# RMS norms with sums by token: root and inverse of 128x5, and rows made from the column by the identity

## The reference

```python
def rmsnorm(x, g):
    y = x * lax.rsqrt(jnp.mean(x * x, axis=-1, keepdims=True) + EPS)
    return y * g

def trunk_layer(x, pe, ...):
    h = x + 0.5 * rmsnorm(swiglu(rmsnorm(x, f1_pre), f1_up, f1_down), f1_post)
    mix, new = token_mix(rmsnorm(h, m_pre), ...)
    h = h + rmsnorm(mix, m_post)
    h = h + 0.5 * rmsnorm(swiglu(rmsnorm(h, f2_pre), f2_up, f2_down), f2_post)
    e = pe @ ple_w
    return h + rmsnorm(e * jax.nn.sigmoid(rmsnorm(h, ple_pre) @ ple_gate_w), ple_post), new
```

## Time and profile before

| | us |
|---|---|
| median of 3 runs | 3309.02 (3308.73 to 3309.1) |
| the profiled execution's own time | 3304.53 |
| its span | 3302.8 |
| mean granted TensorE clock | 0.975 |
| TensorE busy, matmuls / weight loads | 3122.4 / 2985.0 |
| VectorE / ScalarE / GpSimd busy | 1243.8 / 1110.9 / 1215.3 |
| norm sums L610, the group with `sq` | 86.2 in 260 instructions |
| reciprocals of norms L787 | 62.9 in 32 instructions |

### The profile page before, as it was taken

How to read it: one execution, slowest core, us unless ns; L and a number is a source line. 1 busy time by engine, 2 the same in 40 slices (tenths; PEclk the granted TensorE clock), 3 DMA queues, 4 the chain that set the end, 5 groups by cost and what they waited for, 6 DMA issues and landing times.

```text
span 3302.8 us, 55137 instructions
## 1 busy us (share of the span) xinstructions
PE 3122.4 (95%) x23487; PEld 2985.0 (90%) x23487; DVE 1243.8 (38%) x1435; ACT 1110.9 (34%) x1544; POOL 1215.3 (37%) x564
## 2 busy tenths in 40 slices
PE   8999989899999899999899999898999998999988
PEld 7999989886799899998899999888867998999977
DVE  4332134744443433212443221349344424332134
ACT  3333232235433333323433322322354333333233
POOL 5433442231143433344343334423212434333433
PEclk9999999999999999999999999999999999999998
DMA  3222222221122122232112222122211221222221
GB/s 107 83 83 80 82 59 65 73 74 47 39 77 81 54 83 83 81 89 68 58 58 84 81 81 85 54 66 72 68 47 45 77 82 52 83 83 87 82 63 48
DMA packets 455954, 236.22 MB, mean 72 GB/s; under 512 B 18630, under 2 KB 454150, under 8 KB 455814
## 3 DMA queue, kind: packets, MB, share of 16 engines
q1 hardware_dynamic: 445792, 227.05, 23.5%
q10 hardware_dynamic: 10022, 7.15, 0.7%
HBM read 228.53 MB, written 5.63 MB: 71 GB/s over the span
## 4 chain that ended last, share of the span: by engine, by line
PE 85%; DVE 8%; ACT 3%; POOL 1%; issue 1%; ACTq 1%; POOLq 0%; DVEq 0%
PE ps L585 77%; PE ps L610 3%; DVE ps L787 2%; PE ps L1487 1%; DVE uf L799 1%; PE ps L1505 1%; PE ps L1467 1%; DVE u_lo L793 1%; POOL wlo L1932 1%; POOL u_lo L793 1%; ACT u_hi L715 0%; DVE kgate L1099 0%; DVE roots L1143 0%; PE ps L1491 0%; DVE uf L816 0%
## 5 line engine op out<-in xcount | busy, mean ns | idle before, releaser
L1932 POOL TENSOR_TENSOR wlo<-wraw,whi 128x1024 fp32r<-128x1024 f32 x432 | 1078.8, 2497 | 1922.8 <-ACT whi L552 1922.3
L585 PE MATMUL ps<-u_hi,whi 128*128 128x288 f32 x4800 | 1052.8, 301 | 50.0 <-DVE u_lo L793 27.0
L585 PE MATMUL ps<-u_lo,whi 128*128 128x288 f32 x4800 | 1034.6, 297 | 0.0
L585 PE MATMUL ps<-u_hi,wlo 128*128 128x288 f32 x4800 | 1034.5, 297 | 0.0
L585 PEld LDWEIGHTS ps<-u_hi,whi 128*128 128x128 f32 x4800 | 778.1, 191 | 83.0 <-issue 53.7
L585 PEld LDWEIGHTS ps<-u_lo,whi 128*128 128x128 f32 x4800 | 780.6, 190 | 0.0
L585 PEld LDWEIGHTS ps<-u_hi,wlo 128*128 128x128 f32 x4800 | 780.1, 190 | 0.0
L552 ACT ACTIVATE whi<-wraw 128x1024 fp32r<-128x1024 f32 x432 | 457.3, 1059 | 947.1 <-PE ps L585 946.6
L842 DVE TENSOR_TENSOR sq<-sq,ps 128x576 f32<-128x576 f32 x88 | 66.4, 754 | 750.9 <-PE ps L585 750.9
L585 PE MATMUL ps<-s_hi,whi 128*128 128x288 f32 x1408 | 302.0, 296 | 0.0
L585 PE MATMUL ps<-s_lo,whi 128*128 128x288 f32 x1408 | 301.5, 296 | 0.0
(11 more groups left out here) (268 smaller groups left out, 2585.2 us busy)
## 6 DMA issues: line engine op xcount, KB each, us to landing
wraw<-in_ffn_up SPq DMA_DIRECT2D x176, 512.0 KB, 3.8
wraw<-in_w_in SPq DMA_DIRECT2D x104, 512.0 KB, 3.8
wraw<-in_ffn_down SPq DMA_DIRECT2D x64, 512.0 KB, 4.0
wraw<-in_ffn_down SPq DMA_DIRECT2D x32, 384.0 KB, 3.4
wraw<-in_w_out SPq DMA_DIRECT2D x16, 512.0 KB, 4.1
wraw<-in_ple_gate_w SPq DMA_DIRECT2D x16, 512.0 KB, 4.0
wraw<-in_w_branch SPq DMA_DIRECT2D x16, 256.0 KB, 2.7
xtok<-in_x_prompt SPq DMA_DIRECT2D x4, 512.0 KB, 7.2
```

Source lines behind the costliest of these rows:

```text
L585: ins = pe.matmul(ps[:, 2 * p + f, 0:HT], wt[:, part, w], x[:, k, HT * f:HT * f + HT], start=start and n == 0 and c == 0, stop=stop and n ...
L1932: pool.tensor_tensor(wlo[:, i % SPLIT, :], wraw[:, i % RAW, :], whi[:, i % SPLIT, :], ALU.subtract).then_inc(w_split, 1)
```

## The change

**Sums.** The squares become the weights, in five blocks of 128 tokens (the last one overlaps the fourth by 64), and the moving operand is one column of ones. The sum of a token comes out on its own partition: 128x5 in a corner of the norm's PSUM pair (`token_sums`, `sum_at`). **Root and inverse.** ScalarE takes the root of 128x5 into `rcol`, VectorE its reciprocal. **Rows.** TensorE waits for that (`rstd_ready`) behind two matmuls of `keep_clock`, and `spread` multiplies, block by block, the column repeated 128 times as weights by the identity, which puts the factors of all tokens on each partition; VectorE waits for them (`factors_out`) and applies them as before. The fillers of a pre norm are 2 and 6 in place of 10, of a post norm 2 and 8 in place of 8 (2 alone where the very first norm is formed, none in `N_F2POST` and `N_PPRE`).

**Recurrence.** Both tiles' sums come first, with `headcol`, two columns that each hold ones for one head; then one unit-part of filler products, the factors of both tiles (20 matmuls), and three parts of filler products. The convolution's transposes wait for the finished output `hg_done` and no longer for the root. **Convolution.** The variance is summed by token, and its rows are made after the first quarter of the gate unit. The window attention's transposes wait for the applied norm, not for the root. **Start.** ScalarE copies and scales the gains and rows (`rows_scalar`, eight activations) behind its squares.

The diff, cut to its core:

```diff
-            dve.wait_ge(turned, KD + 1)
-            n = [KD]
-
-            def link(ins):
-                n[0] += 1
-                ins.then_inc(placed, 1)
-                dve.wait_ge(placed, n[0])
-
-
-            link(dve.tensor_copy(gains_all[:].rearrange("p n l k -> p (n l k)"), ps[:, ROW_BANKS[0], 0:128]))
-            for q in (N_F1POST, N_F2POST):
-                g = gains_all[:, q, :, :]
-                link(dve.tensor_scalar(g, g, 0.5, None, ALU.mult))
...
+        def rows_scalar(act):
+
+            act.wait_ge(turned, KD + 1)
+            g = gains_all[:].rearrange("p n l k -> p n (l k)")
+            rows = ps[:, ROW_BANKS[0], 0:128].rearrange("p (n x) -> p n x", n=8)
+            for n0, n1, c in ((N_F1PRE, N_F1POST, 1.0), (N_F1POST, N_MPRE, 0.5), (N_MPRE, N_F2POST, 1.0), (N_F2POST, N_PPRE, 0.5), (N_PPRE, 8, 1.0)):
+                act.activation(g[:, n0:n1], rows[:, n0:n1], ACT.Copy, scale=c).then_inc(rows_kept, 1)
+            act.activation(taps_all[:].rearrange("p l w -> p (l w)"), ps[:, ROW_BANKS[1], 0:N_TAPS], ACT.Copy).then_inc(rows_kept, 1)
+            act.activation(rows_all[:, 0:N_ROWS - 4], ps[:, ROW_BANKS[2], 0:N_ROWS - 4], ACT.Copy).then_inc(rows_kept, 1)
+            act.activation(lb_work[:, 0:4], ps[:, ROW_BANKS[2], N_ROWS - 4:N_ROWS], ACT.Copy).then_inc(rows_kept, 1)
+            act.wait_ge(rows_kept, 8)
...
-            def norm_sums(pe, n, x, start, stop):
-                for f in range(2):
-                    ins = pe.matmul(ps[:, 2 * norm_pair(n) + f, 0:HT], ones[:], x[:, HT * f:HT * f + HT], start=start, stop=stop)
-                    if stop:
-                        ins.then_inc(norm_sum, 1)
+            def sum_at(p):
+
+                return ps[:, 2 * p + 1, 256:256 + TB]
+
+            def token_sums(pe, p, x, start, stop):
+                for tb in range(TB):
+                    t0 = min(128 * tb, T - 128)
+                    ins = pe.matmul(sum_at(p)[:, tb:tb + 1], x[:, t0:t0 + 128], ones[:, 0:1], start=start and tb == 0,
+                                    stop=stop and tb == TB - 1, skip_group_check=True)
                 return ins
 
+            def spread(pe, p, col, to=slice(0, 128)):
+
+                for tb in range(TB):
+                    t0, n0 = 128 * tb, 0 if tb < TB - 1 else 64
+                    ins = pe.matmul(flat(p)[to, t0:t0 + 128 - n0], col(tb), ident[:, n0:128], start=True, stop=True)
+                return ins
+
+            def norm_factors(pe, n):
+                if n != N_F2POST:
+                    keep_clock(pe, 2, 2 if n % 2 else 6)
+                pe.wait_ge(rstd_ready, n + 1 + before(rstd_ready))
+                spread(pe, norm_pair(n), lambda tb: rcol[:, tb:tb + 1].to_broadcast([128, 128])).then_inc(factors_out, 1)
+
             def pe_norm_y(pe, n):
 
                 pe.wait_ge(sq_added, 7 * n + 7 + before(sq_added))
-                norm_sums(pe, n, sqsum, True, False)
+                token_sums(pe, norm_pair(n), sqsum, True, False)
                 pe.wait_ge(sq_ready, 8 * n + 8 + before(sq_ready))
-                norm_sums(pe, n, sq[:, 1, :], False, True)
+                token_sums(pe, norm_pair(n), sq[:, 1, :], False, True).then_inc(norm_sum, 1)
+                norm_factors(pe, n)
                 if n not in (N_F1PRE, N_F2POST):
                     keep_clock(pe, 8, 2)
 
             def h_sums(pe, n, k):
                 pe.wait_ge(sq_ready, 8 * n + k + 1 + before(sq_ready))
-                ins = norm_sums(pe, n, sq[:, k % 2, :], k == 0, k == KD - 1)
-                if k < KD - 1:
-                    ins.then_inc(sq_added, 1)
+                token_sums(pe, norm_pair(n), sq[:, k % 2, :], k == 0, k == KD - 1).then_inc(sq_added if k < KD - 1 else norm_sum, 1)
 
             def pe_norm_h(pe, n):
 
                 for k in range(KD):
                     h_sums(pe, n, k)
-                keep_clock(pe, 10, 6)
+                norm_factors(pe, n)
+                keep_clock(pe, 6, 6)
...
-                for f in range(2):
-                    act.wait_ge(norm_sum, 2 * n + f + 1 + before(norm_sum))
-                    x = ps[:, 2 * norm_pair(n) + f, 0:HT]
-                    act.activation(x, x, ACT.Sqrt, bias=eps_col[:], scale=1.0 / D).then_inc(std_ready, 1)
+                act.wait_ge(norm_sum, n + 1 + before(norm_sum))
+                act.activation(rcol[:], sum_at(norm_pair(n)), ACT.Sqrt, bias=eps_col[:], scale=1.0 / D).then_inc(std_ready, 1)
...
             def dve_rstd(dve, n):
-                for f in range(2):
-                    dve.wait_ge(std_ready, 2 * n + f + 1 + before(std_ready))
-                    x = ps[:, 2 * norm_pair(n) + f, 0:HT]
-                    link(dve, dve.reciprocal(x, x))
-
+                dve.wait_ge(std_ready, n + 1 + before(std_ready))
+                dve.reciprocal(rcol[:], rcol[:]).then_inc(rstd_ready, 1)
+                dve.wait_ge(factors_out, n + 1 + before(factors_out))
...
-                    dve.scalar_tensor_tensor(out=halves(uf[:, k, :]), in0=halves(h[:, k, :]), scalar=gains_all[:, n, L, k:k + 1],
-                                             in1=pair(norm_pair(n)), op0=ALU.mult, op1=ALU.mult).then_inc(u_full, 1)
+                    dve.scalar_tensor_tensor(out=uf[:, k, :], in0=h[:, k, :], scalar=gains_all[:, n, L, k:k + 1],
+                                             in1=flat(norm_pair(n)), op0=ALU.mult, op1=ALU.mult).then_inc(u_full, 1)
...
-            def hg_norm_pe(pe, c):
+            def hg_norm_sums(pe, c):
+
                 pe.wait_ge(hg_sq, 2 + before(hg_sq))
-                ones_product(pe, 2 + c, headones[:], sq[:, c, :]).then_inc(hg_ss, 1)
+                for tb in range(TB):
+                    t0 = min(128 * tb, T - 128)
+                    ins = pe.matmul(ps[:, 5 + 2 * c, 256 + 2 * tb:258 + 2 * tb], sq[:, c, t0:t0 + 128], headcol[:], start=tb == 0,
+                                    stop=tb == TB - 1, skip_group_check=True)
+                ins.then_inc(hg_ss, 1)
+
+            def hg_norm_factors(pe, c):
+                pe.wait_ge(hg_rstd, c + 1 + before(hg_rstd))
+                for a2 in range(2):
+                    ins = spread(pe, 2 + c, lambda tb: rhead[:, c, tb, a2:a2 + 1].to_broadcast([128, 64]), head(a2))
+                ins.then_inc(hg_norm, 1)
...
-                    lk(dve.reciprocal(rstd[:], (std, sqsum)[c][:]))
+                    dve.reciprocal(rhead[:, c], rhead[:, c]).then_inc(hg_rstd, 1)
+                for c in range(2):
+                    dve.wait_ge(hg_norm, c + 1 + before(hg_norm))
                     x = of[:, 2 + c, :]
-                    lk(dve.scalar_tensor_tensor(out=x, in0=x, scalar=rows_all[:, 6 * DEPTH + L:6 * DEPTH + L + 1], in1=rstd[:], op0=ALU.mult, op1=ALU.mult))
+                    lk(dve.scalar_tensor_tensor(out=x, in0=x, scalar=rows_all[:, 6 * DEPTH + L:6 * DEPTH + L + 1], in1=flat(2 + c), op0=ALU.mult, op1=ALU.mult))
                     dve.tensor_tensor(x, x, proj[:, G_ + c, :], ALU.mult).then_inc(hg_done, 1)
                 dve.wait_ge(hg_done, 2 + before(hg_done))
 
 
             def pe_conv(pe):
                 pe.wait_ge(cache_in, CACHE_SHORT + before(cache_in))
-                pe.wait_ge(hg_std, 2 + before(hg_std))
+                pe.wait_ge(hg_done, 2 + before(hg_done))
...
-                for t0, t1 in ((0, SEQ), (SEQ, T)):
-                    for c in range(2):
-                        ins = pe.matmul(flat(3)[:, t0:t1], ones[:], sq[:, c, t0:t1], start=c == 0, stop=c == 1)
+                for c in range(2):
+                    ins = token_sums(pe, 3, sq[:, c, :], c == 0, c == 1)
                 ins.then_inc(cv_var, 1)
-                pe_kept_gate(pe, GATES_CONV - 1)
+                g = GATES_CONV - 1
+                pe_gate_free(pe, g)
+                for j in range(4):
+                    unit_part(pe, U0_GATE + g, j, g % 2, QUARTERS)
+                    if j == 0:
+                        pe.wait_ge(cv_rstd, 1 + before(cv_rstd))
+                        spread(pe, 3, lambda tb: rcol[:, tb:tb + 1].to_broadcast([128, 128])).then_inc(cv_fac, 1)
...
-                pe.wait_ge(cv_std, 1 + before(cv_std))
+                pe.wait_ge(cv_norm, 2 + before(cv_norm))
...
-                    hg_norm_pe(pe, c)
-                    pe_fill(pe, 2)
+                    hg_norm_sums(pe, c)
+                pe_fill(pe, 1)
+                for c in range(2):
+                    hg_norm_factors(pe, c)
+                pe_fill(pe, 3)
...
+                pe.wait_ge(rstd_ready, N_PPRE + 1 + before(rstd_ready))
+                spread(pe, norm_pair(N_PPRE), lambda tb: rcol[:, tb:tb + 1].to_broadcast([128, 128])).then_inc(factors_out, 1)
```

More of the change, by code:

```diff
@@ L144, in trunk @@
         roots = keep("roots", [2 * T])
-        std, rstd = roots[:, 0:T], roots[:, T:2 * T]
+        rcol = keep("rcol", [TB])
+        rhead = keep("rhead", [2, TB, 2])
+        headcol = keep("headcol", [2])
         u_at = keep.at
@@ L738, in act_ffn @@
                         act_round(act, k - (KD - 2))
```

(5 more changed lines are left out.)

34 lines of the change are left out of this document (21 added, 13 removed).

## The result

The changed kernel takes 3335.27 us in the median of 4 runs (3333.8 to 3340.34), the kernel before 3308.88 in the same comparison: a ratio of 1.0088, 95% interval 1.0076 to 1.0100 (ratios here are reckoned from the runs themselves and differ a little from the quotient of the medians, 1.0080). 3335 us had been forecast. Two executions among all that follow, 10011 us of the kernel before and 11135 of wide_posts_by_rows, took more than three times as long as the others, and the ratios leave them out.

A forecast was written before the change was run, and what follows sets the result against it. TensorE, busy 95% of the span and holding 85% of the chain, was taken as the bound. Terms 20.8 - 7.2 + 12 + 2.6 - 0.8 - 1.0 = +26.4 us gave a 3335 us median; range 3262 to 3352.

The forecast's parts named there:

- Which clock: TensorE's clock during the new sums: forecast at half, giving +26 us in total instead of -38.
- The sum of one tile: Ten one-column instructions with 128-column loads on TensorE: 1.10 us at full clock, 2.13 at half.
- break-even of 1.38 us a tile: Time of one sum tile at which a norm ahead of products neither gains nor loses.
- pre norms: Five ordinary norms ahead of products: 21.8 us apply to apply instead of 17.62, +4.15 each, +20.8 us.
- post norms: Eight norms whose factors go into a residual: -0.9 us each, -7.2 us.
- PPRE: Two norms ahead of the embedding gate, sums taking turns with other products: +6 us each, +12 us.
- recurrence: Two recurrence norms: TensorE's own queue takes the place of VectorE's, +1.3 us each, +2.6 us.
- convolution: Two convolution norms: VectorE's long reciprocal goes, rows delay the gate unit; -0.4 us each, -0.8 us.
- start: First norm and setup: the gains' scaling moves off VectorE, -1.0 us.
- The clock stays up: Rival, chance 0.30: full clock in the sums, 1.10 us a tile, pre norm 14.5 us, total 3271 us.
- The clock falls, but one-column instructions keep a pitch of 0.11 us: Rival, chance 0.15: loads in the sums stay fast at half clock, pre norms -1.5 us each, total 3293 us.
- No overlap: Rival, chance 0.05: loads don't overlap one-column instructions, 1.9 to 2.9 us a tile, total 3370 us and more.

The follow-up runs named there:

- wide_posts_by_rows: wide_sums with the eight post norms summed, rooted and inverted by rows as before the change; 3308.95 us, ratio 1.0004 against the kernel before.
- wide_sums: The changed kernel with 96 moving columns of ones in place of 1 in RMS and convolution sums by token; 3281.29 us, ratio 0.9925 against the kernel before.

## Why the prediction was right

The two steps that decided the sign held, and the runs show their cause. **Which clock**: the one-column sums ran at 0.50 from 466 on, and the same loads with 96 columns at 1.00. One premise of this step did not hold: I had the clock's fall already due from the idleness ahead of the sums, but 0.66 us of that was left, and the sums began at 1.00. **The sum of one tile**: 1.03 us at full clock (1.10 forecast) and 2.13 at half (3311.63 to 3313.76, clock 0.50; 2.13 forecast). The break-even of 1.38 us a tile was passed on the far side by the change, and on the near side by wide_sums at 1.18.

By the terms, in the traces (their whole difference is 35.8 us; the recurrence is taken from the pre norm's apply to the transposes of z, the convolution from its variance sums to the first score of window attention):

| term | forecast | trace |
|---|---|---|
| pre norms | +20.8 | +18.4 |
| post norms | -7.2 | -8.1 |
| PPRE | +12 | +17.3 |
| recurrence | +2.6 | +5.4 |
| convolution | -0.8 | +1.7 |
| start | -1.0 | -1.7 |
| stages that the change leaves alone | 0 | +2.8 |

*Pre norms.* +4.8, +4.8, +2.6, +2.6, +3.7 us where +4.15 was said. Fillers, root, inverse and rows at half clock took 482.65 - 479.39 = 3.3 us from the sums' end, 3.6 forecast. The spread comes from when the clock falls, since the eight sums take between 13.96 and 16.36 us: in the changed kernel's second trace the same five norms take 21.34, 21.27, 20.38, 22.23 and 21.75 us.

*Post norms.* Three of the eight took 4.23 or 4.24 us from first sum to apply, a gain of 1.96 where 1.7 was forecast for full clock; three took 4.8 to 5.3. Behind the embedding gate it was 5.95 and 7.52, against 6.24 before: in the last one sums and rows both ran at half clock and the norm lost 1.3 us. The mean gain was 1.0 us, 0.9 forecast.

*PPRE.* The step that was furthest off. I let the first round run at full clock and took a value near that case, 6 us; only the first group did. It started 5.0 us behind the residual's apply in layer 1 where I had 3.3, the groups came at 11.4, 21.2 and 30.0 where I had 8.4, 16.7 and 25.2, and the tail took 3.1 (3.2 forecast). It was +9.5 and +7.8, near the upper bound of 10, and +7.4 and +12.2 in the second trace, the latter beyond it. (That bound was mis-subtracted: 38.7 - 28.04 is 10.7. And with all three terms at their bounds the sum gives 3312 to 3357 us, not 3315 to 3352. Neither matters to the result.)

*Recurrence.* I had the end of the fillers at 16.9 us; it came at 16.7 (611.63 against 594.91). But I gave VectorE 2.6 us for history, copies and products of z, and it took 4.5, of which 2.0 are the one small product that ran beside GpSimd's subtraction. *Convolution.* The clock fell in the sums there too: the rows took 1.91 us, and I had reckoned them at 1.2 with products beside them at full speed. ScalarE's activation of the applied norm came 7.51 us behind the sums where it had come 7.73 behind them, so the norm itself gained 0.2. But the unit of gates on TensorE ended 11.5 us behind the sums in place of 8.7, ScalarE waited 1.20 us for it, and the first score of window attention came 15.6 us behind the sums in place of 14.7. I had named this path, and priced it too low.

So the total of the median, +26.4 against +26.4 forecast, is better than its parts, and that it agrees to a microsecond is luck. PPRE, recurrence and convolution came 10.6 us above the forecast, pre norms, post norms and the start 4.0 below it, and the stages left alone added 2.8. By the traces, on which the terms were built, the sum was 9.4 us too low (3340.34 us against the 3330.9 forecast for a profiled execution). The medians hide this only because the profiled execution of the kernel before happened to lie 4 us below its median and that of the changed kernel 5 above.

*The rivals.* "The clock stays up" was the case of wide_sums: 14.5 us for a pre norm was forecast for it and 14.48 measured; its total was 10 us too low (3271 against 3281), from PPRE, the mixers and the post norms. The Trainium skill ("TensorE: Matmul & The Clock Gate", Part 1, "What's actually happening") lets the clock follow how busy TensorE has been. Here a stretch in which it loaded weights for 9.40 of 9.40 us stood at 0.50, and one with the same loads for 9.23 of 9.37 us under 96 columns each at 1.00. "The clock falls, but one-column instructions keep a pitch of 0.11 us": 80 loads took 16.31 us, and 2.13 us from tile to tile at half clock is 0.213 a load. The Trainium skill's price of a load by its columns alone ("TensorE: Matmul & The Clock Gate", Part 2, "LDWEIGHTS (loading the stationary operand)") holds at full clock, 0.103 us here, and not at half. "No overlap" is out by the same rows.

## What to carry to other kernels

A matmul with hardly any moving columns behind a full weight load was cheap here only while TensorE's clock was up, and in each of the five runs of 80 such instructions it fell. More columns under the same loads cost little (1.12 us for ten instructions of 96 columns, 455.12 to 456.24 in wide_sums, against 1.03 for ten of one column) and can be worth more than the work they add: 96 instead of 1 took 54 us off. Before counting what a shorter operation on VectorE saves, look at what TensorE does in that time, and at the idle stretch ahead of the next block: closing 5.25 us of it made sums faster that nobody had touched. Where a new wait for a result is put on TensorE's queue, ask which small transposes stand behind it that another engine needs, and what the other engine's late work will then run beside.
